# Nested loops of sixteen expert blocks, a last step cut into halves, and ones at other places

## The chip, the cores and the metric

The kernel runs on one core of a Trainium2 chip. The metric is the device time of one execution in microseconds (us), as the median of several runs of the same program on the same inputs; lower is better. The core has five engines with instruction streams of their own, which meet only through semaphores: TensorE (PE), VectorE (DVE), ScalarE (ACT), GpSimd (POOL) and SyncE (SP, which here only issues transfers). On each engine a sequencer reads the stream; register operations and branches are done by the sequencer alone, and the trace shows them with a "q" behind the engine's name (DVEq, and PEldq for TensorE).

## The reference

Two transformer layers over 256 tokens of width 1024, float32. The first has three kinds of attention and merges them through gates. The second has a short convolution and an attention over selected keys (64 per query), and then a mixture of 64 experts of which each token takes 8. What matters here is its end:

```python
x = x + gate1 * mix
h2 = rms_norm_2(x, norm2_g) * (1 + scale2) + shift2
x = x + gate2 * moe(h2, ...)

# moe: scores -> 8 experts per token -> tokens sorted by expert in blocks of at most 128
def expert_block(args):
    e, toks, gs = args
    xb = t[toks]
    return swiglu(xb, w1[e], w3[e], w2[e]) * gs[:, None]
routed = segment_sum(out.reshape(rows, D), row_tok, num_segments=n_tok)
```

## The kernel before, in words

The kernel is written without a scheduler: one order of steps, `SCHEDULE`, is made in Python, and every engine's stream walks that list and emits its own part of each step, with semaphore waits written out. Up to the router there are no loops on the chip.

The steps that the change touches there:

- `make_schedule` appends the second layer's steps. `take(k)` appends the next k products of the second layer's input projection, `("proj2", c, t)`, in the order c = 0, 1, 2, 3, 5, 4, 6, 7 and t = 0, 1. `("topk", t)` selects the keys and `("rope", 1)` rotates queries and keys; both are DVE work alone. After a projection's step comes its `drain`, in which an engine empties the PSUM bank, and before the drain of t = 1 the `split` steps of the next weights: ACT rounds a quarter of the weights (`w_hi`), DVE or POOL forms the rest (`w_lo`, L1255). The drain of c = 5 is a copy on ACT; DVE has nothing in it.
- `turn_branch` i transposes the output of attention branch i for its product with the branch weights: four transposes for each half t of the tokens (L1823), which ACT copies out to `OT` (L1063). For i < 3 both halves go through one bank, `turn_b`, so that PE waits for ACT's copy of half 0 ahead of half 1.
- `KEEP_BUSY` names steps ahead of which PE multiplies a tile of ones by itself (L1718), into a projection bank whose contents are not needed. The result is not used. Each count of the table is one product of 128x128, and two MATMUL records in the trace. A key ("flip", n) stands ahead of the wait of transposing head n's probabilities; a key ("flip", n, g) stands inside, between the units g-1 and g of the head, ahead of the wait for ACT's copy (L1110). ("index", h) stands ahead of the wait of the h-th product of the key selection (L1893, L1894).

The experts are a loop on the chip, since the number of blocks, `n_work`, is known only after the router; in these inputs it is 33, and it can be at most `MAX_WORK` = 79. Each engine loops over turns of `BODY` = 4 blocks and asks ahead of each block whether there is one left:

```python
with dve.Fori(0, -(-MAX_WORK // BODY)) as m4, dve.If(n_work > m4 * BODY):    # L1651: 20 turns
    for r in range(BODY):
        i = m4 * BODY + r
        with dve.If(n_work > i):                                             # L1654
```

The loop can't be left early: turns without a block are still counted through, each with its own question. PE has block 0 ahead of the loop and counts the others (L2091, `MAX_WORK - 1` in turns of four, 20 turns; its question per block is L2094). ACT (L1148), POOL (L907) and SP (L766) have such loops of their own.

In a block, PE forms the up products (L2037, 24 passes), transposes the next block's gathered rows (L2014), adds the block before into the four result banks (`scatter`, L2022: each half of the columns is two token tiles times two parts of y), transposes h (L2052), and forms the down products (L2064). ACT rounds weights, rows, h and y (L1138, L1155, L1133, L1166, L1174); DVE forms the rests: `down_lo` L1658, `up_lo` L1631, h L1663, `x_block_lo` L1625, `h_lo` L1666, and `y_lo` L1675, the last of the block. POOL gathers the rows of the block after next.

After its loop PE scatters the last block, both halves, and then a product of one element by ones (L2101) sets `experts_summed`. DVE waits for it after its own loop, and then takes, tile by tile and half by half, result times gate into `qn` (L1684) and adds that to x (L1687), each addition waiting for its product. SP stores each tile of 128 tokens, 512 KB, when both of its halves are added (L776), and waits for both stores.

Of the kernel before, what the change touches and what calls it, by code (L numbers as in the profile page):

```python
# [30 lines left out]
P = 128  # L31
# [220 lines left out]
def make_schedule():  # L252
# [27 lines left out]
    s.extend(("topk", t) for t in range(NT))  # L280
    s.append(("rope", 1))
    take(5)
# [76 lines left out]
for _it in SCHEDULE:  # L359
# [10 lines left out]
    if _it[0] == "turn2":  # L370
# [10 lines left out]
KEEP_BUSY = {("start",): 16, ("half", "proj", 2, 0): 9, ("proj", 2, 0): 5, ("flip", 16): 5, ("turn_branch", 2): 6,  # L381
             ("xturn", 1, 0): 4, ("xturn", 1, 1): 16, ("proj2", 0, 0): 4, ("turn2", 0, 3, 0): 9, ("turn2", 1): 2,
             ("flip", 30): 4, ("turn_branch", 3): 3, ("out2", 0, 0): 4, ("route", 0): 4, ("route", 1): 5, ("ranks",): 8,
             ("tokens", 0): 4}

BODY = 4
UP, DOWN = 2 * KT * ED, FT * DM
# [8 lines left out]
def build(nc, a, out):  # L396
    ctx = ExitStack()
    with ctx:
# [244 lines left out]
        def _(sp):  # L643
# [279 lines left out]
        def _(act):  # L923
# [17 lines left out]
            for it in RESULTS:  # L941
# [112 lines left out]
                if it[0] == "turn_branch":  # L1054
                    i = it[1]
                    dst = OT if i < 3 else a_parts[0][:, WK:2 * WK, :]
                    for t in range(NT):
                        k = TURN[it + (t,)]
                        act.wait_ge(S("turned"), k + 1)
                        if i in (1, 2) and t == 0:  # L1060
# [3 lines left out]
                                       (rows_b[t] if i == 3 else turn_b)[:, :].rearrange("p (b n) -> p b n", b=4), ACT.Copy,  # L1064
# [114 lines left out]
        def _(dve):  # L1179
# [471 lines left out]
            with dve.Fori(0, -(-MAX_WORK // BODY)) as m4, dve.If(n_work > m4 * BODY):  # L1651
                for r in range(BODY):
                    i = m4 * BODY + r
                    with dve.If(n_work > i):  # L1654
                        nxt = (r + 1) % BODY
                        for f in range(FT):
                            dve.wait_ge(S("down_hi"), 2 * i + f + 1)
                            dve.tensor_tensor(down_lo[:, f, :], raw[:, 1 - r % 2][:, UP + f * DM:UP + (f + 1) * DM],  # L1658
                                              down_hi[:, f, :].bitcast(F32), ALU.subtract).then_inc(S("down_lo"), 1)
                        for m in range(2):  # L1660
                            rest_of_up_weights(i + 1, nxt, 0, m)
                        dve.wait_ge(S("silu_done"), i + 1)
                        dve.tensor_tensor(he, hs[:, 0, :], hidden_b[:, ED:2 * ED], ALU.mult).then_inc(S("h_done"), 1)  # L1663
                        rest_of_rows(i + 1)
                        dve.wait_ge(S("h_hi_ready"), i + 1)
                        dve.tensor_tensor(h_lo[:, :, :], turned_b[:, 0:ED].rearrange("p (f n) -> p f n", f=FT),  # L1666
                                          h_hi[:, :, :].bitcast(F32), ALU.subtract).then_inc(S("h_lo_ready"), 1)
                        take_tokens(i + 2, (r + 2) % BODY)
                        for m in range(2):
                            rest_of_up_weights(i + 1, nxt, 1, m)  # L1670
                        for hf in range(2):

                            dve.wait_ge(S(f"y_hi_{hf}"), i + 1)
                            c = slice(hf * CH, (hf + 1) * CH)
                            dve.scalar_tensor_tensor(out=y_lo[:, c], in0=y_b[hf][:, :], scalar=gcol[:, r, 0:1],  # L1675
                                                     in1=y_hi[:, c].bitcast(F32), op0=ALU.mult, op1=ALU.subtract)\
                               .then_inc(S(f"y_lo_{hf}"), 1)

            dve.wait_ge(S("experts_summed"), 1)
            for t in range(NT):  # L1680
                for hf in range(2):
# [9 lines left out]
        def _(pe):  # L1691
# [18 lines left out]
            begun = 0  # L1710

            def keep_busy(it, ps=None):

                count = KEEP_BUSY.get(it, 0)
                if count and ps is None:
                    ps = use_bank(begun)
                for _ in range(count):
                    pe.matmul(ps[:, 0:P], ones[:, :], ones[:, :], start=True, stop=True)  # L1718

            for it in SCHEDULE:  # L1720
                kind0 = it[0]
                if kind0 == "start":
# [374 lines left out]
            for hf in range(2):  # L2097
                mm = scatter(hf, n_work)
# [60 lines left out]
```

## Time and profile before

| | us |
|---|---|
| runs | 1074.34, 1072.80, 1071.74 |
| median | 1072.80 |
| the profiled execution, its own time | 1076.69 |
| its span, first to last instruction | 1074.8 |
| PE / DVE / ACT / POOL busy | 1014.2 / 789.3 / 585.0 / 288.2 |
| mean granted PE clock | 0.984 |

The span is what the trace shows; 1.9 us lie around it. Busy time of an engine doesn't count what its sequencer does alone. A granted clock of 1.00 is 2.4 GHz and 0.50 is 1.2 GHz. In a row of the timeline the first number is the start, the second the duration of the merged instructions, and in brackets at the end stand the idle time of the engine ahead of them and what ended it.

### The profile page before, as it was taken

The numbers are of one execution on the slowest core, as the hardware profiler recorded it, in microseconds if no ns is written. First come the engines' busy times: TensorE is split into PE (matmuls) and PEld (weight loads), VectorE is DVE, ScalarE is ACT, GpSimd is POOL, SyncE is SP. The second block draws the span as 40 slices with busy tenths as digits, with TensorE's granted clock in tenths as the row PEclk, the third lists the DMA queues.
The fourth block names the chain that finished last, engine by engine and source line by source line (L and its number), as shares of the span: only waits on it lengthen the run. The fifth ranks groups of instructions, "written<-read, shape, count | busy, mean of one in ns | idle before, by whom it ended". The sixth has DMA issues, their size and how long they took to land. (4 is left out here: it accounts for less than half of the span.)

```text
span 1074.8 us, 16509 instructions
## 1 busy us (share of the span) xinstructions
PE 1014.2 (94%) x5138; PEld 816.2 (76%) x5138; DVE 789.3 (73%) x1310; ACT 585.0 (54%) x895; POOL 288.2 (27%) x355
## 2 busy tenths in 40 slices
PE   8999999999999999989979989999999999999993
PEld 7778877788776675777758876788888788888882
DVE  4677887677744543566785645999999999999994
ACT  4555555335434341444425424777777777777771
POOL 5154442124100000041136113333223223323320
PEclk9999999999999999999989999999999999999996
DMA  9876866758535243536242217888888888888871
GB/s 318 280 262 230 259 229 233 253 176 307 169 98 178 92 157 117 168 91 222 91 144 92 98 59 287 299 331 341 307 331 343 316 307 338 329 310 340 337 305 59
DMA packets 85061, 247.37 MB, mean 230 GB/s; under 512 B 13245, under 2 KB 23926, under 8 KB 71699
## 3 DMA queue, kind: packets, MB, share of 16 engines
q1 hardware_dynamic: 70754, 201.19, 52.2%
q0 software_dynamic: 13680, 45.13, 11.7%
q8 instruction: 28, 0.46, 0.2%
q10 hardware_dynamic: 576, 0.41, 0.1%
q14 instruction: 23, 0.18, 0.1%
HBM read 244.27 MB, written 2.29 MB: 229 GB/s over the span
## 5 line engine op out<-in xcount | busy, mean ns | idle before, releaser
L1782 PE MATMUL bank<-w_hi,a_hi 128*128 128x512 f32 (+2 forms) x512 | 206.6, 403 | 9.9 <-DVE w_lo L1255 4.4
L1782 PE MATMUL bank<-w_hi,a_lo 128*128 128x512 f32 (+2 forms) x512 | 197.4, 385 | 0.0
L1782 PE MATMUL bank<-w_lo,a_hi 128*128 128x512 f32 (+2 forms) x512 | 197.2, 385 | 0.0
L1255 DVE TENSOR_TENSOR w_lo<-ring,w_hi 128x1024 fp32r<-128x1024 f32 (+2 forms) x132 | 152.7, 1182 | 52.7 <-ACT w_hi L978 48.5
L978 ACT ACTIVATE w_hi<-ring 128x1024 fp32r<-128x1024 f32 (+2 forms) x140 | 141.1, 1023 | 79.4 <-PE bank L1782 74.9
L1631 DVE TENSOR_TENSOR up_lo<-raw_weights,up_hi 128x1024 fp32r<-128x1024 f32 x136 | 164.5, 1250 | 3.0
L1138 ACT ACTIVATE up_hi<-raw_weights 128x1024 fp32r<-128x1024 f32 x136 | 135.7, 1049 | 0.2 <-DMA raw_weights<-in_w_dram 0.2
L1782 PEld LDWEIGHTS bank<-w_hi,a_hi 128*128 128x128 f32 x512 | 97.0, 189 | 40.8 <-issue 19.0
L1782 PEld LDWEIGHTS bank<-w_hi,a_lo 128*128 128x128 f32 x512 | 97.1, 190 | 19.9
L1782 PEld LDWEIGHTS bank<-w_lo,a_hi 128*128 128x128 f32 x512 | 97.2, 190 | 18.2 <-issue 1.4
L2037 PE MATMUL bank<-up_hi,x_block_hi 128*128 128x512 f32 x264 | 104.3, 395 | 1.0 <-issue 1.0
L2037 PE MATMUL bank<-up_hi,x_block_lo 128*128 128x512 f32 x264 | 104.4, 396 | 0.0
L2037 PE MATMUL bank<-up_lo,x_block_hi 128*128 128x512 f32 x264 | 104.3, 395 | 0.0
L918 POOL TENSOR_SCALAR put<-block_rows,consts 128x256 fp32r<-128x256 f32 x33 | 30.6, 926 | 248.0 <-PE bank L2022 128.1
L809 POOL DMA_DIRECT2D merged<-in_w_ada_dram x96 | 53.3, 558 | 132.3 <-DVE ada_acc L1394 98.6
L789 POOL TENSOR_SCALAR mean_squares<-mean_squares 128x8 f32<-128x8 f32 (+2 forms) x32 | 10.0, 312 | 285.7 <-ACT logits L931 204.2
L1658 DVE TENSOR_TENSOR down_lo<-raw_weights,down_hi 128x1024 fp32r<-128x1024 f32 x66 | 77.9, 1222 | 7.1 <-ACT down_hi L1155 7.0
L2022 PE MATMUL bank<-y_hi,put 128*128 128x512 f32 x132 | 58.5, 444 | 9.0 <-issue 9.0
L1394 DVE SCALAR_TENSOR_TENSOR ada_acc<-merged,c_col,ada_acc 128x512 f32<-128x512 f32 x84 | 62.8, 748 | 4.9 <-DMA merged<-in_w_ada_dram 1.9
L1155 ACT ACTIVATE down_hi<-raw_weights 128x1024 fp32r<-128x1024 f32 x66 | 66.1, 1050 | 0.3 <-issue 0.3
L1174 ACT ACTIVATE y_hi<-bank,block_gates 128x512 fp32r<-128x512 f32 x66 | 45.5, 690 | 31.3 <-PE bank L2064 31.3
L2037 PEld LDWEIGHTS bank<-up_hi,x_block_hi 128*128 128x128 f32 x264 | 49.6, 188 | 13.0 <-issue 1.2
(262 smaller groups left out, 1937.9 us busy)
## 6 DMA issues: line engine op xcount, KB each, us to landing
raw_weights<-in_w_dram SPq DMA_DIRECT2D x102, 1024.0 KB, 6.9
ring<-in_w_in_dram SPq DMA_DIRECT2D x58, 1024.0 KB, 5.8
merged<-in_w_ada_dram POOLq DMA_DIRECT2D x96, 256.0 KB, 4.2
ring<-in_w_out_dram SPq DMA_DIRECT2D x8, 1024.0 KB, 5.3
ring<-in_w_branch_dram SPq DMA_DIRECT2D x6, 1024.0 KB, 4.8
bias<-rel_rows SPq DMA_DIRECT2D x40, 128.0 KB, 5.1
block_rows<-place_rows SPq DMA_DIRECT2D x34, 128.0 KB, 8.6
ring<-in_ws_dram SPq DMA_DIRECT2D x2, 1024.0 KB, 4.9
```

The lines of the kernel that those rows point to most:

```text
L809: gp.dma_start(ada_row(q), src).then_inc(S(f"ada_loaded_{q % ADA_SLOTS}"), 16)
L978: act.activation(w_parts[0][:, 2 * p:2 * p + 2, 0:w], view(j, kind)[:, 2 * p:2 * p + 2, :], ACT.Copy)\
L1138: act.activation(up_hi[:, r % 2, 4 * kh:4 * kh + 4, m, :], raw_up(raw[:, 1 - r % 2, :], kh, m), ACT.Copy)\
L1155: act.activation(down_hi[:, f, :], raw[:, 1 - r % 2][:, UP + f * DM:UP + (f + 1) * DM], ACT.Copy)\
L1174: act.activation(y_hi[:, hf * CH:(hf + 1) * CH], y_b[hf][:, :], ACT.Copy, scale=gcol[:, r, 0:1])\
L1255: dve.tensor_tensor(w_parts[1][:, 2 * p:2 * p + 2, 0:w], view(JOB[it[1:3]], kind)[:, 2 * p:2 * p + 2, :], w_parts[0][:, 2 * p:2 * p + 2, 0 ...
L1394: dve.scalar_tensor_tensor(out=o, in0=ada_row(q), scalar=c_col[:, 1, k:k + 1], in1=o, op0=ALU.mult, op1=ALU.add) .then_inc(S("ada_step" if ...
L1631: dve.tensor_tensor(up_lo[:, r % 2, 4 * kh:4 * kh + 4, m, :], raw_up(raw[:, 1 - r % 2, :], kh, m), up_hi[:, r % 2, 4 * kh:4 * kh + 4, m, : ...
L1658: dve.tensor_tensor(down_lo[:, f, :], raw[:, 1 - r % 2][:, UP + f * DM:UP + (f + 1) * DM], down_hi[:, f, :].bitcast(F32), ALU.subtract).th ...
L1782: mm = pe.matmul(ps[:, 0:wide], a_parts[za][:, k, t * P:(t + 1) * P], w_parts[zw][:, k, 0:wide], start=start, stop=stop)
L2022: mm = pe.matmul(acc_b[2 * t + hf][:, :], put[:, t * P:(t + 1) * P], part[:, hf * CH:hf * CH + CH], start=False, stop=False, skip_group_ch ...
L2037: mm = pe.matmul(hidden_b[:, :], (xe_hi, xe_lo)[zx][:, k, :], (up_hi, up_lo)[zw][:, r % 2, k].rearrange("p m n -> p (m n)"), start=(k == 0 ...
```

## The change

- DVE's loop gets PE's form: block 0 ahead of it, the others counted from 1. On DVE and PE the loop becomes two: an outer one of turns of `LONG` = 16 blocks with its question, and in it one of four parts of `BODY` = 4 blocks. 78 blocks are 5 outer turns.
- PE sets `experts_summed` with the last matmul of each half; the product by ones goes. DVE takes half 0 of both tiles first, products ahead of the additions, then half 1. SP stores four pieces of 256 KB, half 0 of both tiles first.
- `turn_branch` 2 uses two banks, one per half of the tokens, as `turn_branch` 3 does.
- ("rope", 1) moves one `proj2` step later.
- `KEEP_BUSY`: new ("flip", 10, 2): 4, ("flip", 15, 2): 4, ("index", 0): 4, ("index", 2): 4; ("flip", 16) from 5 to 4; ("turn_branch", 2) from 6 to 8. Ones are left out where the bank that they would write has not been drained in the schedule.

```diff
     s.extend(("topk", t) for t in range(NT))
+    take(1)
     s.append(("rope", 1))
-    take(5)
+    take(4)
     s.append(("turn2", 1))
...
 BODY = 4
+LONG = 4 * BODY
...
-            for t in range(NT):
-                sp.wait_ge(S("out_ready"), 2 * t + 2)
-                sp.dma_start(out[0, t * P:(t + 1) * P, :], x[:, t, :]).then_inc(S("out_stored"), 16)
-            sp.wait_ge(S("out_stored"), 16 * NT)
+            for hf in range(2):
+                c = slice(hf * CH, hf * CH + CH)
+                for t in range(NT):
+                    sp.wait_ge(S("out_ready"), 2 * hf + t + 1)
+                    sp.dma_start(out[0, t * P:(t + 1) * P, c], x[:, t, c]).then_inc(S("out_stored"), 16)
+            sp.wait_ge(S("out_stored"), 16 * 2 * NT)
...
-                                       (rows_b[t] if i == 3 else turn_b)[:, :].rearrange("p (b n) -> p b n", b=4), ACT.Copy,
+                                       (rows_b[t] if i >= 2 else turn_b)[:, :].rearrange("p (b n) -> p b n", b=4), ACT.Copy,
...
-            with dve.Fori(0, -(-MAX_WORK // BODY)) as m4, dve.If(n_work > m4 * BODY):
-                for r in range(BODY):
-                    i = m4 * BODY + r
+            expert_block(0, 0)
+            with dve.Fori(0, -(-(MAX_WORK - 1) // LONG)) as turn, dve.If(n_work > turn * LONG + 1), \
+                    dve.Fori(0, LONG // BODY) as part:
+                for b in range(BODY):
+                    i = turn * LONG + (part * BODY + (b + 1))
                     with dve.If(n_work > i):
...
+                        expert_block(i, (b + 1) % BODY)
...
-            dve.wait_ge(S("experts_summed"), 1)
-            for t in range(NT):
-                for hf in range(2):
-                    tmp = qn[:, hf, :]
-                    o = x[:, t, hf * CH:hf * CH + CH]
-                    dve.tensor_tensor(tmp, acc_b[2 * t + hf][:, :], gate_bc[:, 1, hf * CH:hf * CH + CH], ALU.mult)\
...
+            for hf in range(2):
+                c = slice(hf * CH, hf * CH + CH)
+                dve.wait_ge(S("experts_summed"), hf + 1)
+                for t in range(NT):
+                    if hf:
+                        dve.wait_ge(S("out_ready"), t + 1)
+                    dve.tensor_tensor(qn[:, t, :], acc_b[2 * t + hf][:, :], gate_bc[:, 1, c], ALU.mult)\
                        .then_inc(S("final_step"), 1)
-                    dve.wait_ge(S("final_step"), 2 * t + hf + 1)
-                    dve.tensor_tensor(o, o, tmp, ALU.add).then_inc(S("out_ready"), 1)
+                for t in range(NT):
+                    dve.wait_ge(S("final_step"), 2 * hf + t + 1)
+                    dve.tensor_tensor(x[:, t, c], x[:, t, c], qn[:, t, :], ALU.add).then_inc(S("out_ready"), 1)
...
+                    if ("drain",) + BANKED[begun - 2] not in passed:
+                        return
                     ps = use_bank(begun)
...
-                        if i < 3 or t == 0:
+                        if i < 2 or t == 0:
                             turn_bank(TURN[it + (t,)])
-                        ps = rows_b[t] if i == 3 else turn_b
+                        ps = rows_b[t] if i >= 2 else turn_b
...
-            with pe.Fori(0, -(-(MAX_WORK - 1) // BODY)) as m4, pe.If(n_work > m4 * BODY + 1):
+            with pe.Fori(0, -(-(MAX_WORK - 1) // LONG)) as turn, pe.If(n_work > turn * LONG + 1), \
+                    pe.Fori(0, LONG // BODY) as part:
                 for b in range(BODY):
-                    i = m4 * BODY + (b + 1)
+                    i = turn * LONG + (part * BODY + (b + 1))
                     with pe.If(n_work > i):
-                        expert_block(i, (b + 1) % BODY, m4 + 1 + (b + 2) // BODY)
+                        expert_block(i, (b + 1) % BODY, turn * (LONG // BODY) + (part + (1 + (b + 2) // BODY)))
             pe.wait_ge(S("put_ready"), n_work)
             for hf in range(2):
-                mm = scatter(hf, n_work)
-            mm.then_inc(S("block_done"), 1)
-
-            pe.matmul(y_b[0][0:1, 0:1], ones[:, 0:1], ones[:, 0:1], start=True, stop=True).then_inc(S("experts_summed"), 1)
+                scatter(hf, n_work).then_inc(S("experts_summed"), 1)
```

## Rows read from the trace of the kernel before

**Rows 1.** By stretch: length, busy PE PEld DVE ACT POOL, granted clock, DMA share, GB/s

```profile
1041.20:1052.70 11.50, 11.45 (x56) 9.24 (x55) 10.56 (x15) 8.97 (x12) 3.44 (x4) 1.00 0.40 155
1053.20:1062.10 8.90, 0.00 (x0) 0.00 (x0) 1.28 (x2) 0.69 (x1) 0.00 (x0) 0.69 0.21 59
```

**Rows 2.** Timeline of the end, PE, DVE and SP's stores

```profile
1053.94 0.75 DVE L1675 SCALAR_TENSOR_TENSOR y_lo<-bank,block_gates,y_hi 128x512 fp32r<-128x512 f32 x1 [0.21 <-ACT y_hi L1174]
...
1062.15 0.77 PE L2022 MATMUL bank<-y_hi,put 128*128 128x512 f32 x1 [8.96 <-issue]
...
1066.05 0.69 DVE L1684 TENSOR_TENSOR qn<-bank,gate_bc 128x512 f32<-128x512 f32 x1 [11.36 <-PE bank L2101]
1066.78 0.69 DVE L1687 TENSOR_TENSOR x<-x,qn 128x512 f32<-128x512 f32 x1
1067.39 0.68 DVE L1684 TENSOR_TENSOR qn<-bank,gate_bc 128x512 f32<-128x512 f32 x1
...
1068.83 3.00 SPq L776 DMA_DIRECT2D out_dram<-x  x2
...
1070.76 0.69 DVE L1687 TENSOR_TENSOR x<-x,qn 128x512 f32<-128x512 f32 x1
```

**Rows 3.** One line's sequencer records, PE's loop, 1050.4 to 1062: durations in ns, first and last start

```profile
L2091 PEldq FUSED_REGOPS  x12: 44/44/50, 1050.6 to 1061.2; - x12
```

**Rows 4.** The same for DVE: its loop from 1055, its question per block from 1050

```profile
L1651 DVEq FUSED_REGOPS  x11: 44/44/51, 1055.1 to 1062.2; - x11
...
L1654 DVEq ALU_OP  x3: 40/40/40, 1054.0 to 1054.5; - x3
```

**Rows 5.** Timeline of blocks 30 to 32: DVE, and PE's transposes of h

```profile
1031.51 2.36 DVE L1658 TENSOR_TENSOR down_lo<-raw_weights,down_hi 128x1024 fp32r<-128x1024 f32 x2 [0.20 <-ACT down_hi L1155]
...
1036.06 0.42 DVE L1663 TENSOR_TENSOR hT<-hs,bank 128x256 f32<-128x256 f32 x1
...
1037.04 0.39 PE L2052 MATMUL bank<-consts,hT 128*128 128x128 f32 x2
...
1043.09 2.36 DVE L1658 TENSOR_TENSOR down_lo<-raw_weights,down_hi 128x1024 fp32r<-128x1024 f32 x2 [0.23 <-ACT down_hi L1155]
```

**Rows 6.** One line's sequencer records, ACT's loop, 1052 to 1075

```profile
L1148 ACTq ALU_OP  x12: 35/35/35, 1054.0 to 1060.5; - x12
```

**Rows 7.** Issue to landing of the two stores of the result

```profile
out_dram<-x SPq DMA_DIRECT2D x2, 512.0 KB, 2.6
```

**Rows 8.** Timeline around `turn_branch` 2

```profile
405.76 1.56 PE L1718 MATMUL bank<-ones 128*128 128x128 f32 x12
...
408.17 0.66 PE L1823 MATMUL bank<-consts,O 128*128 128x128 f32 x4 [0.85 <-DVE O L1470]
...
409.51 0.66 PE L1823 MATMUL bank<-consts,O 128*128 128x128 f32 x4 [0.69 <-ACT OT L1063]
...
410.94 1.54 PE L1801 MATMUL bank<-ring,OT 128*128 128x512 f32 x2 [0.78 <-ACT OT L1063]
```

**Rows 9.** Timeline, PE at heads 10, 15 and 16, and at the key selection

```profile
253.01 0.52 PE L1905 MATMUL bank<-consts,logits 128*128 128x128 f32 x3 [1.39 <-ACT probsT L1110]
...
349.93 0.52 PE L1905 MATMUL bank<-consts,logits 128*128 128x128 f32 x3 [1.51 <-ACT probsT L1110]
350.29 1.28 PE L1718 MATMUL bank<-ones 128*128 128x128 f32 x10
...
504.80 0.50 PE L1893 MATMUL bank<-T 64*128 64x128 f32 x4 [0.37 <-ACT T L1078]
...
506.29 0.48 PE L1893 MATMUL bank<-T 64*128 64x128 f32 x2 [0.57 <-ACT relu L1089]
```

**Rows 10.** Busy time by stretch, columns as in rows 1: where the granted clock was low

```profile
254.40:257.80 3.40, 3.40 (x17) 3.40 (x18) 3.37 (x10) 1.62 (x2) 0.00 (x0) 0.51 1.04 389
411.40:414.80 3.40, 3.40 (x5) 1.31 (x4) 0.00 (x0) 0.00 (x0) 0.00 (x0) 0.51 1.02 406
507.00:510.40 3.40, 3.40 (x11) 2.27 (x9) 1.25 (x3) 0.00 (x0) 1.84 (x2) 0.50 1.05 402
```

More of the change, by code:

```diff
@@ L379 @@
 BRANCHED = [it for it in BANKED if it[0] == "branch"]
[L381 to L384, printed above, removed]
+KEEP_BUSY = {("start",): 16, ("half", "proj", 2, 0): 9, ("proj", 2, 0): 5, ("flip", 10, 2): 4, ("flip", 15, 2): 4,
+             ("flip", 16): 4, ("turn_branch", 2): 8, ("xturn", 1, 0): 4, ("xturn", 1, 1): 16, ("proj2", 0, 0): 4,
+             ("turn2", 0, 3, 0): 9, ("index", 0): 4, ("index", 2): 4, ("turn2", 1): 2, ("flip", 30): 4, ("turn_branch", 3): 3,
+             ("out2", 0, 0): 4, ("route", 0): 4, ("route", 1): 5, ("ranks",): 8, ("tokens", 0): 4}
 BODY = 4
+LONG = 4 * BODY
 UP, DOWN = 2 * KT * ED, FT * DM
@@ L1679, in _, with expert_block @@
-            dve.wait_ge(S("experts_summed"), 1)
-            for t in range(NT):
-                for hf in range(2):
-                    tmp = qn[:, hf, :]
-                    o = x[:, t, hf * CH:hf * CH + CH]
-                    dve.tensor_tensor(tmp, acc_b[2 * t + hf][:, :], gate_bc[:, 1, hf * CH:hf * CH + CH], ALU.mult)\
+            def expert_block(i, r):
+                nxt = (r + 1) % BODY
+                for f in range(FT):
+                    dve.wait_ge(S("down_hi"), 2 * i + f + 1)
+                    dve.tensor_tensor(down_lo[:, f, :], raw[:, 1 - r % 2][:, UP + f * DM:UP + (f + 1) * DM],
+                                      down_hi[:, f, :].bitcast(F32), ALU.subtract).then_inc(S("down_lo"), 1)
+                for m in range(2):
+                    rest_of_up_weights(i + 1, nxt, 0, m)
+                dve.wait_ge(S("silu_done"), i + 1)
+                dve.tensor_tensor(he, hs[:, 0, :], hidden_b[:, ED:2 * ED], ALU.mult).then_inc(S("h_done"), 1)
+                rest_of_rows(i + 1)
+                dve.wait_ge(S("h_hi_ready"), i + 1)
+                dve.tensor_tensor(h_lo[:, :, :], turned_b[:, 0:ED].rearrange("p (f n) -> p f n", f=FT),
+                                  h_hi[:, :, :].bitcast(F32), ALU.subtract).then_inc(S("h_lo_ready"), 1)
+                take_tokens(i + 2, (r + 2) % BODY)
+                for m in range(2):
+                    rest_of_up_weights(i + 1, nxt, 1, m)
+                for hf in range(2):
+                    dve.wait_ge(S(f"y_hi_{hf}"), i + 1)
+                    c = slice(hf * CH, (hf + 1) * CH)
+                    dve.scalar_tensor_tensor(out=y_lo[:, c], in0=y_b[hf][:, :], scalar=gcol[:, r, 0:1],
+                                             in1=y_hi[:, c].bitcast(F32), op0=ALU.mult, op1=ALU.subtract)\
+                       .then_inc(S(f"y_lo_{hf}"), 1)
@@ new lines, in _ @@
+            expert_block(0, 0)
[3 more added lines that the diff above has]
+                    i = turn * LONG + (part * BODY + (b + 1))
+                    with dve.If(n_work > i):
+                        expert_block(i, (b + 1) % BODY)
+            for hf in range(2):
+                c = slice(hf * CH, hf * CH + CH)
[4 more added lines that the diff above has]
+                    dve.tensor_tensor(qn[:, t, :], acc_b[2 * t + hf][:, :], gate_bc[:, 1, c], ALU.mult)\
@@ L1708, in use_bank @@
                 return proj_b[n % 2]
-            begun = 0
+            begun, passed = 0, {("drain",) + it for it in BANKED[-2:]}
             def keep_busy(it, ps=None):
@@ L1721, in _ @@
                 kind0 = it[0]
+                passed.add(it)
                 if kind0 == "start":
```

21 lines of the change are left out of this document (removed).

## The prediction

> **What bounds the kernel now.** I read the page first: PE is busy for 94% of the span, so I looked for the places where it isn't, and only then at the others. Busy time by stretch gives two kinds of time [rows 1]. In a block of the expert loop PE works 11.45 of 11.50 us at full clock: nothing but less PE work or fewer stalls can shorten it, and the change touches neither. In the 8.9 us from 1053.2 PE, ACT and POOL do nothing, and DVE only ends its last `y_lo`. The timeline of the end shows why this is on the path: `y_lo` ends at 1053.94 + 0.75 = 1054.69, PE's last scatter starts at 1062.15 with "issue" as its releaser (it waits for nothing that the profile shows), DVE's first L1684 at 1066.05, and from there DVE and the last store set the end [rows 2]. The sequencer's records of PE's loop name the cause: twelve turns without a block, first records 1050.6 to 1061.2, so 10.6 / 11 = 0.96 us for each [rows 3]. DVE counts through eleven such turns, 1055.1 to 1062.2, 0.71 us each [rows 4]. With 33 blocks and loops for 79, that is what 12 and 11 turns of four amount to.
>
> **Part 1, the loops.** PE: 78 blocks in turns of 16 are 5 turns; blocks 1 to 32 fill two, and 3 stay empty instead of 12. They begin where they began (1050.6, while the last down products still run: PE works until beyond 1052.7, so its sequencer is some 2 us ahead [rows 1, 3]) plus about 0.4 for closing the inner loop, and take 3 x 0.96 = 2.9: PE's stream is free at 1053.9; the same working gives 1062.1 for before. `y_lo` half 0, which had ended when half 1 started at 1053.94, is next late and no later, so the first scatter starts at about 1054.0 instead of 1062.15. DVE: its last `y_lo` starts at 1053.94 as before, and its loop records come right behind that start [rows 4]: its sequencer isn't ahead. Block 32 now closes a part and a turn: the three questions L1654 for blocks that don't exist (from 1054.0, some 0.27 apart, 0.8 us) go, the end of the inner loop comes in (0.2 to 0.4), so the first empty turn begins at 1055.1 - 0.8 + 0.3 = 1054.6, and three take 3 x 0.71 = 2.1. That frees DVE at about 1056.7 (1056.3 to 1057.3) instead of 1055.1 + 11 x 0.71 = 1062.9. So the order of the two engines is turned round: before, DVE waited 3.2 us for PE; now PE is done ahead of DVE.
>
> A page of the Trainium skill, Advanced Engine Details and Errata, section Control Flow Timing, gives about 108 ns for a compare-and-branch. By it an empty turn with its two branches would be some 0.2 us, an estimate, and the eight turns that DVE no longer counts would be worth 1.7 us instead of 8 x 0.71 = 5.7; the trace shows 0.71 and 0.96 for a turn, and the sum goes by the trace.
>
> **Part 2, the last step.** From PE's first scatter matmul to DVE's start were 3.9 us [rows 2], at a clock that had fallen in the idle time [rows 1]. The pause ahead of them is now about 1 us, so I take full clock and half the time: half 0 is summed at 1055.0, half 1 at 1056.0. Both lie ahead of DVE's 1056.7 and cost nothing; if DVE were free at once, they would set its start at 1055.2; at half clock half 0 would still be there at 1056.0. DVE starts at 1056.7, 9.35 us earlier. Its eight instructions: a product and the addition that waits for it are 0.73 apart, one that waits for nothing just issued 0.61 (1066.05, 1066.78, 1067.39) [rows 2]. Before that is 4 x 0.73 + 3 x 0.61 + 0.69 = 5.4; products first, no instruction waits for its direct predecessor: 7 x 0.61 + 0.69 = 5.0, a gain of 0.4. The last store starts when DVE ends: before at 1071.45, now at 1061.7. It took 2.6 us for 512 KB [rows 7] and landed at 1074.05, 0.75 ahead of the span's end. What 256 KB take, no row shows: at most 2.6, at least half, 1.3; I take 2.0, since part of a transfer's time doesn't follow its size and the piece before is issued only 0.6 us earlier. What else could end last: ACT's own loop, unchanged, ends at 1060.5 [rows 6]. The end comes at 1061.7 + 2.0 + 0.75 = 1064.45. Parts 1 and 2 together: 1074.8 - 1064.45 = 10.35; with DVE at 1057.3 and a store of 2.6, 9.15; with 1056.3 and 1.3, 11.4. I take 10.2.
>
> **Part 3, the loops' inside.** Two counters in every wait value may mean more register operations. PE: hidden behind the 2 us by which its sequencer is ahead. DVE: they run while the instruction before is busy, 0.4 to 1.2 us mostly. A turn of the old loop between blocks 31 and 32 shows as 0.23 us of idle time ahead of L1658 against 0.20 without a turn [rows 5]. The inner loop's turn has no question of its own and should cost no more; the outer one's only real turn, ahead of block 17, perhaps 0.3 us once. DVE's margin is at h: L1663 ends at 1036.48, PE takes it up at 1037.04 [rows 5], so 0.3 to 0.5 us of lateness cost nothing. Value: 0, bounds 0 and +0.5. DVE's peeled block 0 is the same instructions at another place.
>
> **Part 4, `turn_branch` 2.** PE no longer waits 0.69 for ACT's copy of half 0 [rows 8]. ACT becomes next: a copy costs PE 0.69 and 0.78 as the two rows show, the transposes of half 0 end at 408.83, and two copies in a row bring the branch product to 408.83 + 2 x 0.69 = 410.2 instead of 410.94: -0.75. The two ones more (0.26 each, since six take 1.56) end at 405.76 + 8 x 0.26 = 407.8, ahead of 408.17, where PE waits for DVE anyway: 0.
>
> **Part 5, the ones.** The granted clock fell to half for 3.4 us at 254.4, 411.4 and 507.0 [rows 10], each time right behind idle time of PE: 1.39 at head 10, 0.85, 0.69 and 0.78 at `turn_branch` 2, 0.37 and 0.57 at the key selection [rows 8, 9]. The change puts ones into all three. Four ones are 1.04 us. At head 10 (gap 1.39) and head 15 (gap 1.51) they fit and cost nothing. At the key selection they don't: 1.04 - 0.37 is up to 0.65 ahead of index 0, and 1.04 - 0.57 up to 0.45 ahead of index 2; I take +0.85 for both (bounds 0.4 and 1.1). One fewer at ("flip", 16): -0.26, since its five end where the next step starts. The low clock: in each of the three stretches PE is busy 3.40 of 3.40 us at half speed, and so does 1.7 us of work; 5.1 in all. One profiled execution can't tell how often it falls there; the runs differ by 2.6 us, one or two such falls. I take that half of the 5.1 is in a median run and goes: -2.5 (bounds 0 and -5.1). DVE's key selection follows PE's index products, so what PE gains ahead of them is passed on. Parts 4 and 5: -0.75 + 0.85 - 0.26 - 2.5 = -2.7; bounds +0.4 and -5.3.
>
> **Part 6, the rotation.** ("rope", 1) moves past ("proj2", 5, 0) and its drain. In these DVE, which alone rotates, has no instruction, and no split stands there. POOL, SP and PE have nothing in "rope". No engine's stream changes: 0. The test of the drain in `KEEP_BUSY` takes none of the ones in the old list away, since each stands behind the drain that it asks for.
>
> **Sum.** 10.2 + 2.7 = 12.9. The profiled execution took 1076.69, so its like would be 1063.8; the median of the runs is 3.9 lower (1072.8), and the parts are work of the engines that the runs have too. 1072.8 - 12.9 = 1059.9.
>
> **Rivals.**
>
> A, as forecast: 87%, 1056.5 to 1063.
>
> B, the tail gains less. The cost of an empty turn in a run without the profiler, or what comes behind the loop on DVE, could be otherwise; a DVE free at 1059 instead of 1056.7, 2.3 less, and no clock gained gives 1072.8 - 7.9 - 0.2 = 1064.7. For it: the median is 3.9 below the profiled execution, and some of that may be the sequencers' time. Against: PE and DVE count turns at even distances, there is nothing else in that idle time. 8%, 1063 to 1066.5.
>
> C, slower. The wait values of two counters put register operations between DVE's instructions that are not hidden. Place: from `down_lo` to h in each block; it decides once DVE is over 0.3 to 0.5 us later there, in 32 blocks. To lose 12.9 us it needs 0.4 us more than that margin, 0.8 us a block, some four or five records at the 0.18 (0.71 / 4) that a record of a turn costs. With 1.0 us: 32 x 0.6 = 19 us, 1079. Against it: in that stretch DVE's instructions of a kind stand without a gap between them, the register operations of today included. 2%.
>
> D, code fetch. Each inner turn or each outer skip jumps over a body of four blocks. Nearest row: PE, with the longer body, needs 0.96 for an empty turn and DVE 0.71, so 0.25 is what the jump over the longer body adds at most. At 8 inner turns and uncovered that is 2.0: 1061.9, inside the range. 2%. The Trainium skill has a rule that speaks for it: Runtime: NRT & Kernel Launch, section Instruction fetch mechanics, says that a taken branch to code outside the pages held stalls for a fetch. The trace's even 0.96 and 0.71 show no such stall.
>
> E, the tail doesn't shorten because another stream ends last: ACT's at 1060.5 leaves 3.8 us. 1%.
>
> **Chances and range.** A difference of over 0.2%, 2.1 us, is about what a measurement can tell. Faster: A, B, D, E: 97%. Same: 1% (C with 0.8 us). Slower: 2%. The range 1056.5 to 1064.0 takes A and half of B.
>
> **What would show it.** After the last `y_lo`: three empty turns on DVE and three on PE, PE's scatter within 0.3 us of `y_lo` half 0 at full clock, DVE's first product with the gate some 2.8 us behind the last `y_lo`'s start, eight instructions 0.61 apart, four stores, the last landing in about 2.0. Idle ahead of L1658 still 0.20 to 0.23, PE busy some 11.45 of 11.50 us in a block. At `turn_branch` 2 no 0.69 gap; DVE's order around "rope" unchanged. Wrong would be: a longer period, gaps behind short DVE instructions, index products later by over 1 us, or a clock that falls at 411 or 507 all the same.

## The result, and the profile after

| | before | after |
|---|---|---|
| median, measured side by side | 1073.57 us (4 runs) | 1063.29 us (4 runs, 1060.7 to 1064.17) |
| ratio, with its 95% interval | | 0.9903 [0.9886, 0.9921] |
| the profiled execution: its own time / its span | 1076.69 / 1074.8 | 1060.70 / 1058.8 |
| mean granted PE clock in it | 0.984 | 0.995 |
| from the start of the last `y_lo` half 1 to the end of the span | 20.9 | 10.3 |

The change is 10.3 us faster (8.5 to 12.2), where 12.9 were forecast. The two profiled executions lie 16.0 apart. 10.6 of that is the tail, 4.6 is the time ahead of block 0 of the experts (its first up product starts at 668.03 before and at 663.46 after), and 0.8 the 33 blocks. The last two compare one execution with one; more on that below.

The end, in the timeline of the changed kernel (start, duration, instruction, idle time ahead and what ended it):

```profile
1047.61 0.74 DVE L1677 SCALAR_TENSOR_TENSOR y_lo<-bank,block_gates,y_hi 128x512 fp32r<-128x512 f32 x1
...
1048.50 0.47 PE L2037 MATMUL bank<-y_hi,put 128*128 128x512 f32 x1 [0.69 <-DVE y_lo L1677]
1048.56 0.75 DVE L1677 SCALAR_TENSOR_TENSOR y_lo<-bank,block_gates,y_hi 128x512 fp32r<-128x512 f32 x1 [0.21 <-ACT y_hi L1178]
...
1050.20 0.40 PE L2037 MATMUL bank<-y_lo,put 128*128 128x512 f32 x1
1051.11 1.29 DVE L1695 TENSOR_TENSOR qn<-bank,gate_bc 128x512 f32<-128x512 f32 x2 [1.79 <-PE bank L2037]
1052.31 1.28 DVE L1699 TENSOR_TENSOR x<-x,qn 128x512 f32<-128x512 f32 x2
...
1054.71 1.28 DVE L1699 TENSOR_TENSOR x<-x,qn 128x512 f32<-128x512 f32 x2
```

Against [rows 2]: PE's scatter starts where `y_lo` half 1 does, and its releaser is now `y_lo`, not "issue". From its start to its end it takes 2.1 us; before, 3.9 us lay between its start and DVE's. DVE starts 2.55 us behind the last `y_lo`'s start instead of 12.1, and its eight instructions take 4.9 instead of 5.4. The idle time ahead of DVE's first product names PE, but PE had ended at 1050.60; the loops' sequencer records say what was late (one line's records each: duration in ns, first and last start; DVE's loop, then PE's, from the last block on):

```profile
L1682 DVEq FUSED_REGOPS  x3: 55/63/63, 1049.1 to 1050.6; - x3
...
L2106 PEldq FUSED_REGOPS  x3: 44/50/50, 1045.5 to 1047.0; - x3
```

Three empty turns each, where [rows 3, 4] had twelve and eleven. DVE's take 0.73 and end at 1051.06, where its first product starts. PE's take 0.75, not the 0.96 of [rows 3], and end before `y_lo` is there.

The same stretch as busy time (length, busy PE PEld DVE ACT POOL, granted clock, DMA share, GB/s), and the stores, issue to landing:

```profile
1048.50:1050.60 2.10, 2.10 (x8) 1.34 (x8) 0.75 (x1) 0.03 (x1) 0.00 (x0) 1.00 0.60 222
```

```profile
out_dram<-x SPq DMA_DIRECT2D x4, 256.0 KB, 2.1
```

Ahead of the experts, PE's gaps at `turn_branch` 2, at heads 10 and 15, and at the key selection [rows 8, 9] in the changed kernel:

```profile
253.13 0.55 PE L1920 MATMUL bank<-consts,logits 128*128 128x128 f32 x3 [0.41 <-ACT probsT L1114]
...
348.40 0.55 PE L1920 MATMUL bank<-consts,logits 128*128 128x128 f32 x3 [0.53 <-ACT probsT L1114]
...
406.66 1.09 PE L1838 MATMUL bank<-consts,O 128*128 128x128 f32 x8 [0.40 <-DVE O L1474]
408.59 3.67 PE L1816 MATMUL bank<-ring,OT 128*128 128x512 f32 x8 [0.83 <-ACT OT L1067]
...
500.10 0.33 PE L1858 MATMUL bank<-consts,rows 128*128 128x128 f32 x1 [0.16 <-ACT T L1082]
500.27 1.06 PE L1732 MATMUL bank<-ones 128*128 128x128 f32 x8
501.25 0.50 PE L1908 MATMUL bank<-T 64*128 64x128 f32 x4
...
503.20 0.50 PE L1908 MATMUL bank<-T 64*128 64x128 f32 x4
...
504.07 0.50 PE L1797 MATMUL bank<-w_hi,a_hi 128*128 128x512 f32 x1
```

1.39 and 1.51 have become 0.41 and 0.53, the 0.69 between the two halves of `turn_branch` 2 is gone, and at the key selection ones stand where the gaps of 0.37 and 0.57 were. The granted clock is 1.00 in all three stretches in which [rows 10] show 0.5:

```profile
253.90:257.30 3.40, 3.40 (x29) 3.07 (x27) 3.37 (x9) 2.08 (x3) 0.00 (x0) 1.00 1.05 399
408.90:415.00 6.10, 6.10 (x15) 2.66 (x14) 1.38 (x2) 0.00 (x0) 0.00 (x0) 1.00 0.74 294
504.00:510.00 6.00, 6.00 (x30) 4.70 (x30) 3.87 (x10) 1.15 (x3) 1.44 (x1) 1.00 0.62 231
```

Inside the loops, the idle time ahead of the first `down_lo` of a block is 0.20, and 0.23 ahead of blocks 8, 12, 16 and so on to 32, as in the kernel before. DVE's parts now end elsewhere, ahead of blocks 5, 9, 13 and so on, and there it is 0.20. So a turn of DVE's inner loop shows nothing, and the 0.23 of [rows 5] was not DVE's turn, as the prediction took it; ACT, which releases `down_lo`, still has its turns at those blocks, but that this is the cause was not tested. The one outer turn with blocks behind it, ahead of block 17, shows as 0.43. Blocks 13, 16 and 17:

```profile
816.15 2.36 DVE L1660 TENSOR_TENSOR down_lo<-raw_weights,down_hi 128x1024 fp32r<-128x1024 f32 x2 [0.20 <-ACT down_hi L1159]
...
851.03 2.36 DVE L1660 TENSOR_TENSOR down_lo<-raw_weights,down_hi 128x1024 fp32r<-128x1024 f32 x2 [0.23 <-ACT down_hi L1159]
...
862.82 2.37 DVE L1660 TENSOR_TENSOR down_lo<-raw_weights,down_hi 128x1024 fp32r<-128x1024 f32 x2 [0.43 <-ACT down_hi L1159]
```

### The profile page after: what moved, and what is told of

Same layout as the page of the kernel before. It is cut to its first block and busy times, and to the rows that moved or that the text cites. A ratio compares the mean times of both kernels' runs of the same rounds, so it can differ in the third digit from the quotient of the medians.

```text
span 1058.8 us, 16493 instructions
## 1 busy us (share of the span) xinstructions
PE 1010.4 (95%) x5170; PEld 815.0 (77%) x5170; DVE 788.8 (74%) x1310; ACT 584.7 (55%) x895; POOL 287.8 (27%) x355
## 5 line engine op out<-in xcount | busy, mean ns | idle before, releaser
L1142 ACT ACTIVATE up_hi<-raw_weights 128x1024 fp32r<-128x1024 f32 x136 | 135.8, 1050 | 0.3 <-DMA raw_weights<-in_w_dram 0.3
L1159 ACT ACTIVATE down_hi<-raw_weights 128x1024 fp32r<-128x1024 f32 x66 | 66.0, 1050 | 0.3 <-issue 0.3
L2052 PEld LDWEIGHTS bank<-up_lo,x_block_hi 128*128 128x128 f32 x264 | 49.6, 188 | 11.9
```

Source lines behind the costliest of these rows:

```text
L1142: act.activation(up_hi[:, r % 2, 4 * kh:4 * kh + 4, m, :], raw_up(raw[:, 1 - r % 2, :], kh, m), ACT.Copy)\
L1159: act.activation(down_hi[:, f, :], raw[:, 1 - r % 2][:, UP + f * DM:UP + (f + 1) * DM], ACT.Copy)\
L2052: mm = pe.matmul(hidden_b[:, :], (xe_hi, xe_lo)[zx][:, k, :], (up_hi, up_lo)[zw][:, r % 2, k].rearrange("p m n -> p (m n)"), start=(k == 0 ...
```

## The experiments

Each group shared its runs of the kernel before; their medians were 1072.69 (22 runs), 1072.88 (29) and 1073.13 (15). In brackets stands the 95% interval of a ratio. 0.001 is 1.07 us. A gain in us is the ratio's; the quotient of two of the medians differs from the ratio by up to 0.0016. The time from block 0's first up product to the last `y_lo` half 1, "the blocks" below, has no trend in the fourteen profiled executions but scatters from 384.0 to 386.4 us, so a difference of 1 us there between two executions says nothing.

### The loops alone

Only the nested loops of DVE and PE (with DVE's block 0 ahead), everything else as before.

> The kernel before with the two nested loops alone (PE's and DVE's, block 0 of DVE ahead); last step, stores, ones and banks as before. By my working PE's stream is free at 1054.0 and DVE's at 1056.7, so the scatter starts 8.1 us earlier, and DVE's last step right behind PE's one-element product: all eight scatter matmuls at full clock end by about 1056.2, so DVE starts at 1056.7, 9.3 us earlier. Theory 1 (nothing inside the loops; ones and banks gain nothing in the median): -9.3 us, ratio 0.9913. Theory 2 (two counters cost 2 to 3 us inside the loops, ones and banks gain 2.7): -6.5 to -7, ratio 0.9937. The trace tells too: from block 0's first up matmul to the last y_lo 385.9 us in the kernel before.

Measured: 1063.19 us, 0.9910 [0.9895, 0.9925], so -9.6. Its DVE starts 2.54 us behind the last `y_lo` and needs 5.4 for the old order:

```profile
1052.14 0.75 DVE L1674 SCALAR_TENSOR_TENSOR y_lo<-bank,block_gates,y_hi 128x512 fp32r<-128x512 f32 x1 [0.21 <-ACT y_hi L1175]
1054.68 0.69 DVE L1691 TENSOR_TENSOR qn<-bank,gate_bc 128x512 f32<-128x512 f32 x1 [1.79 <-PE bank L2109]
...
1059.39 0.69 DVE L1694 TENSOR_TENSOR x<-x,qn 128x512 f32<-128x512 f32 x1
```

The forecast for this part was 9.35. So the loops give what the tail shows, 20.9 - 11.3 = 9.6, and no loss shows inside (the blocks took 385.6 us, before 385.9); the theory that their inside costs 2 to 3 us falls, since its -6.5 to -7 lies outside the interval (-11.3 to -8.1).

### The last step alone

Only `experts_summed` by halves, DVE's order and the four stores.

> The kernel before with the last step, the sums and the stores by halves alone; loops as before. PE's first scatter stays late and at half clock: half 0 is summed some 1.7 us ahead of half 1, and DVE's empty turns end at 1062.9, so DVE starts at about 1064.1 instead of 1066.05 (-1.9), works 5.0 instead of 5.4 (-0.4), and the last store lands in about 2.0 instead of 2.6 (-0.6). Both theories: -2.9 us, ratio 0.9973; if the smaller store gains nothing, -2.3.

Measured: 1068.93 us, 0.9966 [0.9955, 0.9976], -3.7. The trace has -2.7 in the tail: with the old loops PE is still the later one, and DVE no longer waits for both halves. That is inside the interval (-4.8 to -2.6), at its edge.

### The ones and the two banks

```diff
-KEEP_BUSY = {... ("flip", 16): 5, ("turn_branch", 2): 6, ...}
+KEEP_BUSY = {... ("flip", 10, 2): 4, ("flip", 15, 2): 4, ("flip", 16): 4, ("turn_branch", 2): 8, ("index", 0): 4, ("index", 2): 4, ...}
-                        ps = rows_b[t] if i == 3 else turn_b
+                        ps = rows_b[t] if i >= 2 else turn_b
```

> The kernel before with the change's table of ones, the test of the drain, two banks for turn_branch 2 and the rotation's place; loops and last step as before. Theory 1: the clock falls elsewhere as often, 0 to -1 us in the median. Theory 2: -2.7 us, ratio 0.9975. In the profile the granted clock should not fall at heads 10, turn_branch 2 and the key selection, and the index products start up to 0.85 later against the step ahead of them.

Measured: 1070.16 us, 0.9974 [0.9963, 0.9986], -2.8, nearly what the forecast had for parts 4 and 5. But its trace put the gain at the wrong place: block 0 of the experts starts at 663.87, no earlier than where the old ones stand (662.84, below), and the tail is 18.4 us instead of 20.9. The profiled execution of the kernel before starts it at 668.03, but with three falls of the clock ahead of it. PE's twelve empty turns took 0.77 us instead of 0.96, in a loop whose code was the same. That asked for three more kernels.

### Each half of that, and the code moved without work

Two banks alone (the second pair of lines above):

> Of the change only the two banks of turn_branch 2; ones, loops and last step as before. By the working of the prediction -0.75 us: no 0.69 gap ahead of the transposes of half 1, the branch product some 0.75 earlier, ratio 0.9993. Theory 'place' (PE's empty turn costs 0.96 or 0.77 us by where the code of the loop lies, and that made most of what the ones and banks together showed): the code ahead of the loop hardly changes its length here, so the turns stay at 0.96 and the ratio at 0.9993. Theory 'work' (ones and banks together won their 2.7 us ahead of the experts): the banks give 0.75 of it, same number.

Measured: 1071.69 us, 0.9987 [0.9974, 1.0000]. From the first transpose of `turn_branch` 2 to the branch product it is 1.92 us, before it was 2.77 [rows 8]; turns of 0.97.

```profile
406.64 1.09 PE L1823 MATMUL bank<-consts,O 128*128 128x128 f32 x8 [0.85 <-DVE O L1470]
408.56 1.53 PE L1801 MATMUL bank<-ring,OT 128*128 128x512 f32 x3 [0.83 <-ACT OT L1063]
```

The new ones alone (the first pair):

> Of the change only the table of ones, turn_branch 2 with one bank as before, loops and last step as before. Theory 'place': block 0 of the experts starts no earlier than in a run of before whose clock doesn't fall at 254, 411 and 507 (662.9 to 663.2): +0.6 by the longer index stretch, and in the median about -0.6 by falls that go; PE's empty turns at 0.77, -2.1; ratio 0.998. Theory 'work': the gain is ahead of block 0, -2 us by the clock, the turns at 0.96, ratio 0.998 too; the trace tells them apart by the start of the first block and the pitch of the turns.

Measured: 1070.09 us, 0.9968 [0.9956, 0.9981], -3.4. Block 0 starts at 665.21, some 1.5 us later than expected, and the clock fell at 357.2, where it had not been expected:

```profile
357.24:360.64 3.40, 3.40 (x12) 2.37 (x11) 0.48 (x2) 1.47 (x5) 0.00 (x0) 0.50 0.18 62
```

PE had been idle for 0.79 and 0.69 us just ahead of it. The turns take 0.75 us each, as theory 'place' had them.

Then the kernel before, with code ahead of PE's loop that is never run:

```diff
+            with pe.If(n_work > 2 * MAX_WORK):
+                for _ in range(17):
+                    pe.matmul(hidden_b[:, 0:P], ones[:, :], ones[:, :], start=True, stop=True)
             expert_block(0, 0, 1)
```

> The kernel before with 17 products of ones that are never run, in an If whose condition can't hold, in PE's stream ahead of block 0: the code of PE's loop lies as much further on as the 17 ones of the change move it, and no work is added but one question (0.2 to 0.3 us of PE's sequencer, which is ahead). Theory 'place': PE's empty turns take 0.77 instead of 0.96, twelve of them end some 2.1 us earlier, ratio 0.998 to 0.9985. Theory 'work': where code lies costs nothing, turns at 0.96, ratio 1.000 to 1.0003.

Measured: 1073.40 us, 1.0005 [0.9991, 1.0018]. This one did not test what it was made for: with a condition that can't hold, the products are not in the built program, and PE's stream was one instruction longer. It shows only that this much changes nothing. Its trace is of use for something else: for the rest it is the kernel before, the clock fell in it at none of the three places of [rows 10], and its block 0 starts at 663.59, 4.4 us ahead of the 668.03 of the profiled execution of before. With a condition that can hold:

```diff
+            with pe.If(n_work > 60):
```

> The kernel before with 17 products of ones in PE's stream ahead of block 0, in an If that asks n_work > 60, which isn't so here (33), so that they stand in the code and aren't run. The run before it with a condition that can't hold at all had lost them in the build: PE's stream was one instruction longer than before, and its turns took 0.97. Now PE's loop lies 19 instructions further on, against 17 with the new ones, whose turns took 0.74. Theory 'place' (the price of PE's empty turn depends on where the code of the loop lies): turns at about 0.75, the scatter 2.3 to 2.6 us closer to the last y_lo, ratio 0.9976 to 0.9985. Rival (it is the ones that are run, or something else in that kernel): turns at 0.97, ratio 1.000 to 1.0005.

Measured: 1070.05 us, 0.9974 [0.9961, 0.9987], -2.8, a little more than expected, with no work added or taken away but one question ahead of block 0. PE's loop records in this kernel, in the one with the new ones, and in the one whose products the build had left out:

```profile
L2094 PEldq FUSED_REGOPS  x12: 44/44/50, 1048.6 to 1056.9; - x12
```

```profile
L2096 PEldq FUSED_REGOPS  x12: 44/44/50, 1047.0 to 1055.2; - x12
```

```profile
L2094 PEldq FUSED_REGOPS  x12: 44/44/50, 1045.6 to 1056.2; - x12
```

8.3 / 11 = 0.75, 8.2 / 11 = 0.75 and 10.6 / 11 = 0.96. With its code 17 or 19 instructions further on in the built stream, the same loop counts an empty turn 0.21 us faster, and twelve of them make 2.5. In the trace the difference sits at one place of the turn: from a register operation (ALU_OP) to the start of the compare-and-branch behind it it is 0.10 us instead of 0.33, in every turn but the first. The scatter starts 5.6 us behind the last `y_lo` in both moved kernels, instead of 8.2:

```profile
1052.00 0.75 DVE L1675 SCALAR_TENSOR_TENSOR y_lo<-bank,block_gates,y_hi 128x512 fp32r<-128x512 f32 x1 [0.21 <-ACT y_hi L1174]
```

```profile
1057.61 0.77 PE L2022 MATMUL bank<-y_hi,put 128*128 128x512 f32 x1 [6.37 <-issue]
```

So of the 3.4 us of the new ones alone, the code moved without work gives 2.8 (2.6 in the start of the scatter), and 0.6 is left (0.9968 against 0.9974): within the uncertainty nothing. In the changed kernel as a whole the side effect is worth nothing: PE, with three turns, is ahead of `y_lo` anyway, and its turns took 0.75 with the old ones too, and in the kernel with the loops alone.

### The changed kernel with the old ones

```diff
-KEEP_BUSY = {... the new table ...}
+KEEP_BUSY = {... the old table ...}
```

> The changed kernel with the old table of ones; two banks, loops and last step as changed. Against the changed kernel, which measured a ratio of 0.9903: theory 1: the same ratio within 0.001. Theory 2: 2 us slower than the changed kernel, 0.992 to 0.9925, with the granted clock falling again at head 10 or the key selection.

Measured: 1061.34 us, 0.9889 [0.9871, 0.9908]. It was run again later beside the changed kernel itself:

> The changed kernel as it is, again, for a comparison with the old table of ones on the same chip. Earlier 0.9903 [0.9886, 0.9921]; I expect 0.990.

> The changed kernel with the old table of ones, again. By the prediction's working the new ones win 1.9 us (-2.5 for the clock, +0.85 for the key selection, -0.26 for head 16), so this kernel would be at 1.9 us more than the changed one beside it, 0.992. Theory 'rare': a median run of the kernel before has hardly any of the three falls of the clock which its profiled execution shows, the new ones save 0.6 in the mean and cost 0.6, so both kernels are the same within 1 us, 0.990; with the earlier run's 0.9889 the old ones would be 1.5 us the faster.

Measured: changed 1061.60 us, 0.9898 [0.9881, 0.9914]; with the old ones 1061.96 us, 0.9912 [0.9896, 0.9928]. The first time the old ones were ahead by 0.0014 (the changed kernel's 0.9903 comes from the runs of the result), in this group behind by 0.0014. Taken together no difference shows, with an uncertainty of about 2 us; 1.9 us in favour of the new ones had been forecast. PE around the key selection, with the old ones:

```profile
500.48 0.33 PE L1858 MATMUL bank<-consts,rows 128*128 128x128 f32 x1 [0.16 <-ACT T L1082]
501.18 0.50 PE L1908 MATMUL bank<-T 64*128 64x128 f32 x4 [0.37 <-ACT T L1082]
...
502.68 0.48 PE L1908 MATMUL bank<-T 64*128 64x128 f32 x2 [0.57 <-ACT relu L1093]
...
503.91 0.50 PE L1797 MATMUL bank<-w_hi,a_hi 128*128 128x512 f32 x1
```

From the last transpose to the first weight product behind the four index products it is 3.43 us, with the new ones 3.97: they cost 0.54. Block 0 starts at 662.84 with the old ones in this profiled execution and at 663.46 with the new. And the clock did not fall in it, although its gap ahead of 253.35 is the old 1.39:

```profile
254.30:257.70 3.40, 3.40 (x29) 3.07 (x28) 3.37 (x9) 2.07 (x4) 0.00 (x0) 1.00 1.06 401
409.40:415.00 5.60, 5.60 (x15) 2.48 (x14) 1.38 (x2) 0.00 (x0) 0.00 (x0) 1.00 0.78 306
504.00:510.00 6.00, 6.00 (x30) 4.76 (x32) 3.88 (x10) 1.30 (x3) 1.71 (x2) 1.00 0.68 259
```

Over all profiled executions of this study: with the old table the clock fell at 8 of 27 such places (nine kernels, three places each; three of the eight are those of the kernel before), with the new table at none of 15. But it fell elsewhere instead: at 357.2 with the new ones alone, and just ahead of block 0, at 663, in the kernel with ones and banks and in the second execution of the changed kernel; with the old ones once at 481, once at 484 and once at 663. And in every execution it fell near 550 to 557, for 3.4 or for 6.8 us, as here in the changed kernel:

```profile
550.05:556.88 6.83, 4.94 (x23) 4.97 (x24) 5.11 (x6) 0.00 (x0) 0.00 (x0) 0.50 0.38 121
```

All time at the low clock ahead of block 0, added up, is 17.1 us in the kernel before, 8.5 in the mean of the other eight executions with the old table, and 8.2 in the mean of the five with the new one. PE was busy for 7.6 and 6.8 us of the last two, so the new ones save half of 0.8, some 0.4 us.

### The price of an empty turn, and none at all

```diff
-LONG = 4 * BODY
+LONG = 2 * BODY
```

> The changed kernel with LONG = 8 instead of 16: ten outer turns, six of them empty instead of three. DVE's three more empty turns at 0.73 are 2.2 us and PE's at 0.75 the same; both stand on the path, DVE's first product with the gate starts 2.2 us later behind the last y_lo, +2.2 us, ratio 0.9923 if the changed kernel is at 0.9903. If an empty turn were free without the profiler, the time would be the changed kernel's own.

Measured: 1062.66 us, 0.9912 [0.9896, 0.9928], against 0.9898 [0.9881, 0.9914] for the changed kernel beside it: +1.5 by the ratios, 1.1 by the two medians. The uncertainty holds 2.2 and also 0; that empty turns cost time in the median is shown by the loops alone, not by this pair. The trace has the forecast to a tenth. DVE starts 4.68 us behind the last `y_lo`, 2.13 more than in the changed kernel, with "issue" as the releaser, and the tail is 12.4 us instead of 10.3:

```profile
1047.80 0.75 DVE L1677 SCALAR_TENSOR_TENSOR y_lo<-bank,block_gates,y_hi 128x512 fp32r<-128x512 f32 x1 [0.21 <-ACT y_hi L1178]
1052.48 1.29 DVE L1695 TENSOR_TENSOR qn<-bank,gate_bc 128x512 f32<-128x512 f32 x2 [3.94 <-issue]
```

Last, the old ones and loops that end by a count:

```diff
-            with dve.Fori(0, -(-(MAX_WORK - 1) // LONG)) as turn, dve.If(n_work > turn * LONG + 1), \
-                    dve.Fori(0, LONG // BODY) as part:
+            with dve.Fori(0, (n_work + (BODY - 2)) // BODY) as part:
                 for b in range(BODY):
-                    i = turn * LONG + (part * BODY + (b + 1))
+                    i = part * BODY + (b + 1)
...
(and the same for pe)
```

> The changed kernel with the old table of ones, and with loops of PE and DVE that end by a count worked out from n_work, (n_work + 2) // 4 turns of four blocks, so that neither counts through an empty turn; ACT's, POOL's and SP's loops as they are. DVE is free right behind its last y_lo, about 1049.2 instead of 1051.1 in the profile of the changed kernel, half 0 is summed at 1049.6, so DVE's first product with the gate starts at 1049.7: 1.4 us earlier. Against the changed kernel with the old ones (1061.34, 0.9889) that is 1060.0, 0.9876. If the period of a block were shorter too, for want of the second counter, blocks 0 to 32 would take under 385 us; I expect 385 to 386.

Measured: 1059.13 us (1058.36 to 1059.66), 0.9866 [0.9846, 0.9887], -14.4: the fastest kernel of the study, 2.5 below the median of the changed one. Its DVE waits for PE again, 0.39 us:

```profile
1047.79 0.75 DVE L1677 SCALAR_TENSOR_TENSOR y_lo<-bank,block_gates,y_hi 128x512 fp32r<-128x512 f32 x1 [0.21 <-ACT y_hi L1178]
1048.93 1.29 DVE L1694 TENSOR_TENSOR qn<-bank,gate_bc 128x512 f32<-128x512 f32 x2 [0.39 <-PE bank L2036]
```

DVE's start is 1.14 us behind the last `y_lo` instead of 2.55, the tail 8.9 instead of 10.3: 1.4, as expected. In the trace the rest of the 2.5 stands in the blocks, 384.05 us against 385.1 in the changed kernel, where 385 to 386 had been expected; but the two banks alone, with the loops of before, had 384.04 too. So only the 1.4 is shown to be the loops' end. The idle time ahead of block 17 is 0.20 again, without an outer turn.

The rotation's move was not run by itself. In the kernel with the new ones alone, which has it too, DVE's 188 instructions from 440 to 560 come in the order of before.

## Why the prediction was right, and where it was off

The median of 1063.29 lies 3.4 above the forecast 1059.9 and 0.7 inside the upper end of the range. 0.8 of that is the base: 1072.80 was taken, and 1073.57 measured beside the change. The other 2.6 is gain that did not come. By its number alone the result lies in rival B's band, 1063 to 1066.5; the traces show that B's cause, a tail that gains less, was not there, and that the part on the clock was too large.

Part 1, the loops, held. Forecast were three empty turns on each engine, PE's done first, DVE's start 1056.7 - 1053.94 = 2.8 us behind the last `y_lo` and a gain of 9.35; the trace has three, three, 2.55, and the kernel with the loops alone -9.6. One step of it was wrong without effect: PE's turn is 0.75 there, not 0.96, so PE was free 1.06 us ahead of the last `y_lo` and not level with it. The figure of the Trainium skill (Advanced Engine Details and Errata, Control Flow Timing, about 108 ns for a compare-and-branch) does not give the price of a turn: by the prediction's estimate from it, the loops would have gained 4 us less on DVE. In the trace the record of one compare-and-branch lasts 0.21 us on PE and some 0.06 on DVE; a turn has two of them and two register operations, and on DVE most of its 0.71 us lies between these records.

Part 2 held. A scatter at full clock in 2.1 us (2.0 forecast), DVE's eight in 4.9 (5.0), the stores landing in 2.1 (2.0), and from DVE's end to the end of the span 2.8 (2.75). Measured against the kernel with the loops alone, whose tail is 11.3, the last step is worth 1.0, as forecast. Parts 1 and 2 together are 10.6 in the trace, for 10.2.

Part 3 held: 0.43 instead of 0.20 at the one outer turn, for "perhaps 0.3 us once", and no longer idle times elsewhere. Its reading of [rows 5] was wrong without effect: the 0.23 is not DVE's turn.

Part 4: -0.85 in the trace for -0.75; the 0.83 that is left ahead of the branch product is ACT's copy, the 0.78 of before. Measured alone -1.4 (-2.8 to 0).

Part 5 is the term that was mis-sized. The ones at the key selection cost 0.54 there instead of 0.85. But the clock's -2.5, "half of the 5.1 is in a median run", was far too much. Outside the kernel before, eight profiled executions with the old table had 5 falls at the three places of a possible 24, 0.6 for each run, and 0.6 x 1.7 us is 1.1; and even that was not won, since the clock fell elsewhere instead. Over all the time ahead of block 0 the new ones save some 0.4 us. The granted clocks of the runs of before say too that the profiled execution was a rare one: one fall takes 3.4 x 0.5 / 1074.8 = 0.0016 off the mean; it had 0.984, the medians of the three groups 0.989, 0.988 and 0.987, so a median run has about two to three falls fewer, though the mean does not say at which places. In sum the new ones were worth -0.4 + 0.54 - 0.26 = -0.1 by rows, and 0 within the uncertainty of the direct comparison, for a forecast of -1.9. The one execution at hand was among the slowest of its kernel, 3.9 above the median, and the prediction said so when it set its base; it should have taken the falls as the likeliest part of those 3.9 and counted little of them as gain. That the new ones and banks measured -2.8 all the same, for a forecast of -2.7, was luck: most of it came from the moved code.

With the corrected terms the sum is 10.2 + 0.85 + 0.1 = 11.2 instead of 12.9. Measured were 10.3 (8.5 to 12.2) and, later, 10.9 (9.2 to 12.8). What is left, under 1 us, is inside both intervals, and no run here gives it a cause.

Part 6 held, and so did the rivals' ranking. C, registers that slow the loops: no such gaps. D: PE's turn at 0.75 against DVE's 0.71 to 0.73 leaves 0.04 at most for the jump over the longer body; but that where the code lies has a price is shown, 0.21 us for each empty turn of PE. The page that the prediction named for D (the Trainium skill, Runtime: NRT & Kernel Launch, Instruction fetch mechanics) has a stall for a taken branch whose target is not held and must be fetched first; the trace shows some 0.2 us more with every turn of one placement and none with another. Whether it is a fetch, no record here tells. The nearest row had been read wrongly at that point: PE's 0.96 against DVE's 0.71 was, but for 0.04, not the longer body but the place of the code.

## What to carry to other kernels

A loop with a static bound and a question in it is paid for to its last turn, at 0.7 to 1.0 us a turn on the engine that has to do the last step: count the turns behind the last piece of work in the sequencer's records, and end the loop by a count from the data where that is possible (here DVE then began its last step another 1.4 us earlier than with nesting). A fall of the clock in one profiled execution is not a fall in the median: compare that execution's mean clock with the other runs' before its removal is booked as gain, and add up the low clock of the whole stretch, not only at the places that were mended. And when a part of a change gives just what was forecast, look in the trace whether it gives it at the place forecast: the ones and banks met the forecast to 0.1 us, and most of it came from the code being moved.

## What the runs showed of the hardware that was not expected

- The price of an empty turn of the same PE loop depends on where its code lies: 0.96 to 0.98 us in four kernels (before, the last step alone, the banks alone, one instruction more), 0.75 with 17 or 19 instructions more ahead of it (0.77 with ones and banks together). Twelve turns made 2.5 us of the median, 0.9974 [0.9961, 0.9987], without any work changed.
- DVE's empty turn was 0.71 to 0.73 in every one of these kernels, with one loop and with the outer of two.
- At idle times of the same length, 1.39 us among them, the granted clock fell in some executions and not in others: 8 of 27. With the idle times filled it fell at none of 15, but the whole time at the low clock ahead of block 0 stayed at 8.2 us instead of 8.5 (mean of five and of eight executions, the kernel before left out).
